# Eight modulation blocks summed on VectorE ahead of TensorE, and Ln and Exp of two scan directions in one instruction

## The chip, the cores and the metric

The kernel runs on one core of one Trainium2 chip. The metric is the device time of one execution in microseconds; for the kernel before it is the median of three runs, 1372.58 us (1371.57 to 1374.09).

## The reference, cut to what matters

Two layers of a hybrid backbone run over 128 context tokens and 256 sample tokens with shared weights. Each layer takes six modulation vectors from the conditioning, one set for the context tokens and one for the sample tokens:

```
mod = silu(c) @ w_mod[l] + b_mod[l]            # c: (1024,), w_mod[l]: (1024, 6 * 1024); for c and for c_ctx
sh1, sc1, g1, sh2, sc2, g2 = split(mod, 6)
h = rms_norm(x, g_pre_mix) * (1 + sc1) + sh1
x = x + g1 * rms_norm(mixer(h), g_post_mix)
h = rms_norm(x, g_pre_ffn) * (1 + sc2) + sh2
x = x + g2 * rms_norm((silu(gate) * up) @ w_ffn_out, g_post_ffn)    # gate, up = split(h @ w_ffn_in), 2816 each
...
a = exp(log_a);  u = sqrt(-expm1(2 * log_a)) * i * x                # RG-LRU, two directions, width 1024
h_t = a_t * h_{t-1} + u_t
```

All tensors are float32.

## The kernel before

The program lays out one core's whole work by hand: each engine has its own stream, written once for each of two layers, and the engines meet at counting semaphores. `Steps` gives each event a label and `at(engine, label)` the value to wait for.

**Weights.** `plan_loads` lists every weight load in the order in which SP issues it. A load is one tile of 128x1024 (two chunks of 128 rows by 512 columns). A split load goes to one of three `raw` buffers; ScalarE writes its rounded part (`highs`, L1106, to `weight_high`), VectorE the rest (`lows`, L1475, to `weight_low`), five slots each. SP waits for the low of the load three before (L529). TensorE then makes three products per block, high by high (L642), high by low activations (L649) and low by high (L650), for 384 tokens at once. A job such as `fi3` is four loads: eight chunks of four 128-column blocks, into four banks. Jobs alternate between two sets of four banks. `token_job` (`wo` and `fo`) has the tokens stationary (L727 to L729).

**FFN stage.** Jobs `fi0` to `fi10` make gate and up blocks, `fo` the output. ScalarE and VectorE, at the end of job j, run two loads ahead (`highs(..., ahead=2)`, `lows(..., ahead=2)`), then `silu` (L1437), `hid` (L1956), the high of `hid` and `hid_low` (L1946). After that VectorE begins with the low of the third load of job j+1.

**Modulation.** The 6 x 1024 columns of `w_mod` are twelve blocks of 512 (r = 0 to 11). The table `MODS` gives each block a host job. Its weights come in four quarters of two chunks (`mod_weight`, two slots, not split). In a hosting job, after the first and the third load, `mod_products` (L681) puts the two conditioning columns, padded to 32, as stationary side against 128 columns of weights, two quarters at a time, into the 128 columns of the banks that the tokens leave free; the chunks go to four groups of 32 partitions. VectorE copies the banks out (`mod_partial`, L1498), and `mod_fold` (L692) adds the four groups and turns the result into columns, in the third load of a later job (`FOLDED`). Blocks 4, 5, 10 and 11 are the gains g1 and g2: `gain_spread` (L709) spreads them over all partitions as rows, with the bias as one more row that `gain_rows` brings. Blocks 0 to 3 (`NEXT`) are those of the next layer, made in the FFN stage of the layer before (not in layer 1, `hosts`); 10 and 11 are needed at the end of the same stage.

**RG-LRU stage.** For each 128 channels and each direction ScalarE makes `t = exp(2 log a)`, `a = exp(log a)` (L1271, L1272), VectorE `squared_root` = (t + 1) tau (L1704), ScalarE the root as Ln and Exp with scale 0.5 (L1277, L1282), VectorE the scans (`scans`, L1679 to L1693). In `lru_coefficients` round e issues the two exponentials of direction e, the Ln of direction e - 1, the last Exp of direction e - 2, and then, in rounds 1, 3, 5, 7 and 9, the high of a weight load. It runs twice a layer, for channels 0 to 3 and 4 to 7. TensorE meanwhile runs `gg0`, `gg1` with gate blocks between them (L857 to L859), then `m2a` and on.

## Time and profile before

| | |
|---|---|
| median of three runs | 1372.58 us |
| the profiled execution: time, span | 1374.85 us, 1373.0 us |
| mean granted TensorE clock | 0.985 |
| busy: TensorE, VectorE, ScalarE | 1310.7, 737.2, 663.6 us |
| L681, hosted modulation products | 1280 records, 43.2 us busy |
| L1475, weight lows | 282, 319.0 us |
| L1106, weight highs | 282, 273.8 us |
| DMA | 196.27 MB, mean 143 GB/s |

One execution is profiled. Busy is the time in which at least one instruction of the engine runs; matmuls overlap, so the pace of TensorE is read from the distance of starts, not from durations. A row of the timeline gives the start, the time from there to the end of the last of its instructions, and in brackets the idle time ahead of it and what ended that. A matmul of float32 operands leaves two records.

### The profile page before, as it was taken

The page shows a single profiled execution, that of the slowest core. Times are in us where ns is not written, and L with a number is a line of the kernel's source. Part 1 is how long each engine was busy: PE and PEld are TensorE (multiplying, and loading weights), DVE is VectorE, ACT ScalarE, POOL GpSimd, SP SyncE. Part 2 cuts the span into 40 slices and gives each one's busy share as a digit, 9 for nine tenths or more (in the row PEclk, how much of TensorE's full clock was granted, in tenths as well). Part 3 has the DMA queues.
Part 4 walks back from the last instruction along what each step waited for, and adds up shares of the span by engine and source line. Part 5 has one row for each costly group of instructions (what it writes and reads, how often), then busy time and mean ns, then how long its engine had stood idle before and what let it go on. Part 6 is the DMA issues. An engine that isn't in the chain of part 4 may idle for free.

```text
span 1373.0 us, 20857 instructions
## 1 busy us (share of the span) xinstructions
PE 1310.7 (95%) x8171; PEld 1196.0 (87%) x8171; DVE 737.2 (54%) x1306; ACT 663.6 (48%) x1199; POOL 18.2 (1%) x38
## 2 busy tenths in 40 slices
PE   5999999998999999999999989999989999999998
PEld 4898899877879999998789988998777899999886
DVE  2687484753754444333367785747447643444424
ACT  4378864743363333332265878637343633333322
POOL 0000000200000000000000000002000000000000
PEclk9999999999999999999999999999999999999999
DMA  9544545313325555535325444453124253445522
GB/s 340 167 139 128 192 138 189 124 61 123 110 91 189 185 184 180 163 134 185 98 85 154 128 158 155 153 191 136 48 77 152 63 158 124 133 151 178 184 97 73
DMA packets 135061, 196.27 MB, mean 143 GB/s; under 512 B 9730, under 2 KB 68268, under 8 KB 134964
## 3 DMA queue, kind: packets, MB, share of 16 engines
q1 hardware_dynamic: 134964, 194.94, 43.4%
q8 instruction: 65, 1.06, 0.3%
q14 instruction: 32, 0.26, 0.1%
HBM read 193.03 MB, written 1.88 MB: 142 GB/s over the span
## 4 chain that ended last, share of the span: by engine, by line
PE 81%; DVE 8%; ACT 6%; DMA 3%; issue 2%; SPq 0%; DVEq 0%; ACTq 0%
PE bank L642 16%; PE bank L649 16%; PE bank L650 15%; PE bank L727 6%; PE bank L729 6%; PE bank L728 6%; PE bank L681 3%; DVE weight_low L1475 2%; ACT weight_high L1106 2%; PE bank L605 2%; PE bank L1015 1%; PE bank L1039 1%; PE bank L709 1%; DVE lru_h L1683 1%; DMA raw<-in_w_o_mla 1%
## 5 line engine op out<-in xcount | busy, mean ns | idle before, releaser
L649 PE MATMUL bank<-act_low,weight_high 128*128 128x384 f32 x1440 | 490.4, 341 | 1.6 <-DVE weight_low L1475 0.9
L650 PE MATMUL bank<-act_high,weight_low 128*128 128x384 f32 x1440 | 485.2, 337 | 0.0
L1475 DVE TENSOR_TENSOR weight_low<-raw,weight_high 128x1024 fp32r<-128x1024 f32 (+5 forms) x282 | 319.0, 1153 | 251.4 <-ACT weight_high L1106 250.3
L1106 ACT ACTIVATE weight_high<-raw 128x1024 fp32r<-128x1024 f32 (+5 forms) x282 | 273.8, 995 | 298.4 <-DMA raw<-in_w_ffn_in 84.2
L642 PE MATMUL bank<-act_high,weight_high 128*128 128x384 f32 x1440 | 324.2, 346 | 6.6 <-ACT weight_high L1106 4.5
L649 PEld LDWEIGHTS bank<-act_low,weight_high 128*128 128x128 f32 x1440 | 273.9, 190 | 8.9 <-issue 4.2
L650 PEld LDWEIGHTS bank<-act_high,weight_low 128*128 128x128 f32 x1440 | 273.5, 190 | 0.0
L642 PEld LDWEIGHTS bank<-act_high,weight_high 128*128 128x128 f32 x1440 | 256.0, 192 | 17.8 <-issue 9.1
L727 PE MATMUL bank<-weight_high,hid_high 128*128 128x512 f32 x264 | 104.4, 395 | 0.0
L729 PE MATMUL bank<-weight_high,hid_low 128*128 128x512 f32 x264 | 102.8, 389 | 0.0
L728 PE MATMUL bank<-weight_low,hid_high 128*128 128x512 f32 x264 | 102.8, 389 | 0.0
L1956 DVE TENSOR_TENSOR t<-bank,sq 128x384 f32<-128x384 f32 x44 | 24.5, 558 | 123.9 <-PE bank L650 121.0
L1437 ACT ACTIVATE sq<-bank 128x384 f32<-128x384 f32 x44 | 19.3, 490 | 129.7 <-PE bank L650 129.7
L728 PEld LDWEIGHTS bank<-weight_low,hid_high 128*128 128x128 f32 x264 | 49.6, 188 | 11.1 <-issue 1.0
L727 PEld LDWEIGHTS bank<-weight_high,hid_high 128*128 128x128 f32 x264 | 49.6, 188 | 11.1 <-issue 1.0
L729 PEld LDWEIGHTS bank<-weight_high,hid_low 128*128 128x128 f32 x264 | 49.6, 188 | 10.4
L1395 ACT ACTIVATE sq<-bank 128x384 f32<-128x384 f32 (+1 forms) x48 | 20.1, 419 | 64.7 <-PE bank L1024 34.5
L1900 DVE TENSOR_REDUCE negmax<-bank 128x1 f32<-128x384 f32 (+1 forms) x48 | 22.2, 466 | 44.4 <-PE bank L1015 44.1
L681 PE MATMUL bank<-mod_weight,cs 128*32 128x128 f32 x1280 | 43.2, 276 | 0.0
L681 PEld LDWEIGHTS bank<-mod_weight,cs 128*32 128x32 f32 x1280 | 32.5, 109 | 9.9 <-issue 9.9
L1186 ACT ACTIVATE act_high<-t 128x384 fp32r<-128x384 f32 x32 | 16.5, 524 | 48.0 <-DVE t L1545 47.8
L605 PE MATMUL bank<-rstd,x 128*128 128x128 f32 x192 | 30.9, 312 | 8.6 <-ACT rstd L1152 6.8
(221 smaller groups left out, 1512.5 us busy)
## 6 DMA issues: line engine op xcount, KB each, us to landing
raw<-in_w_ffn_in SPq DMA_DIRECT2D x176, 256.0 KB, 3.8
mod_weight<-in_w_mod SPq DMA_DIRECT2D x80, 512.0 KB, 4.8
raw<-in_w_in SPq DMA_DIRECT2D x72, 512.0 KB, 4.3
raw<-in_w_ffn_out SPq DMA_DIRECT2D x44, 512.0 KB, 3.3
first_mod<-in_w_mod SPq DMA_DIRECT2D x4, 2048.0 KB, 14.4
raw<-in_w_o_lru SPq DMA_DIRECT2D x16, 512.0 KB, 3.9
raw<-in_w_out SPq DMA_DIRECT2D x16, 512.0 KB, 3.3
raw<-in_w_o_mla SPq DMA_DIRECT2D x8, 512.0 KB, 6.7
```

The costliest lines, as they stand in the source:

```text
L605: ins = nc.tensor.matmul(turn_bank(job, c)[:, P * a:P * a + P], x[:, a, P * c:P * c + P], rstd[:, P * a:P * a + P], start=True, stop=True)
L642: nc.tensor.matmul(bank(job, g)[:, 0:T], view[0][:, kk, cols], high[:, k, :], start=k == 0, stop=False)
L649: nc.tensor.matmul(o, view[0][:, kk, cols], low[:, k, :], start=False, stop=False)
L650: ins = nc.tensor.matmul(o, view[1][:, kk, cols], high[:, k, :], start=False, stop=k == total - 1)
L681: ins = nc.tensor.matmul(bank(job, b)[32 * q:32 * q + 32, T:512], cs[:, k, :], modw[MIDX[n] % MODR][:, 512 * kk + P * b:512 * kk + P * b + P],
L727: nc.tensor.matmul(o, high[:, k, toks], view[0][:, kk, :], start=k == 0, stop=False)
L728: nc.tensor.matmul(o, high[:, k, toks], view[1][:, kk, :], start=False, stop=False)
L729: ins = nc.tensor.matmul(o, low[:, k, toks], view[0][:, kk, :], start=False, stop=k == 2 * pairs - 1)
L1106: nc.scalar.activation(high, w, ACT.Copy).then_inc(*AC.step())
L1475: nc.vector.tensor_tensor(low, w, high.bitcast(F), ALU.subtract).then_inc(*VE.step())
L1900: nc.vector.tensor_reduce(negmax[:, s % 2:s % 2 + 1], bank("attn", s % 2)[:, 0:n], AX.X, ALU.max, negate=True).then_inc(*VE.step("max", s))
L1956: nc.vector.tensor_tensor(t[c % 2][:, :], bank(f"fi{j}", 2 + g)[:, 0:T], sq[c % 4][:, :], ALU.mult).then_inc(*VE.step("hid", c))
```

## The change

Six blocks leave the list of hosted products: 10 and 11, and 0 to 3 where they are made. Their weights come in the same quarters through the same two slots, three quarters to a job, one behind each of the first three loads of `fi1` to `fi8` (the order is 10, 11, 0, 1, 2, 3; in layer 1 only 10 and 11). VectorE multiplies each chunk of 512 columns by the conditioning value of its row (a scalar for each partition) and adds it to a running total of 128x512, one for each conditioning: four operations a quarter, behind the low of the load in its stream. The totals of 10 and 11 lie in `qkv`, those of 0 to 3 in two halves of `ybuf`, shared by 0 and 2, and by 1 and 3; the first quarter of 2 waits for fold 0, that of 3 for fold 1. TensorE sums over partitions: for the gains `ones` is stationary and the total moves (L709's place); for blocks 0 to 3 each 128 columns of a total are stationary against one column of ones, eight products a fold, in `fi5`, `fi7`, `fi8` and `fi9`. The bias of the gains is added to partition 0 of the totals by VectorE; its rows come with `bias_rows` at the first load of `fi1`.

In `lru_coefficients` the Ln and the last Exp take both directions of a channel block in one instruction of 128x768, in rounds 2, 4, 6 and 8; from round 2 on the first exponential waits for the square that last read its buffer.

```
+MODS = ((6, "qk", "st_qkv"), (7, "gg1", "m2b"), (8, "m2a", "outs"), (9, "m1a", "outs"), (4, "m1b", None), (5, "ol1", None))
+SUMMED = (10, 11, 0, 1, 2, 3)
+SUM_FOLD = {"fi5": 0, "fi7": 1, "fi8": 2, "fi9": 3}
+SUM_AT = {(f"fi{1 + q // 3}", q % 3): (SUMMED[q // 4], q % 4) for q in range(24)}
...
+            if (job, i) in SUM_AT:
+                r, q = SUM_AT[job, i]
+                loads.append(Load(("sum", r), 2, 512, False, [("rows", "w_mod", 2 * q, 2, r * 512, 512, 0)]))
...
+        def total(r, g):
+
+            return qkv_flat[:, 1024 * (r - 10) + 512 * g:1024 * (r - 10) + 512 * g + 512] if r >= 10 else \
+                y_flat[:, 1024 * (r % 2) + 512 * g:1024 * (r % 2) + 512 * g + 512]
...
+                def bias_rows():
+
+                    sp.wait_ge(*at(PE, "spread", 5, 1))
+                    sp.sem_inc(sync_passed, 1)
+                    for r in GAINS["ffn"]:
+                        sp.dma_start(partial[r - 10][0:1, :], A["b_mod"][l:l + 1, 512 * r:512 * r + 512]
+                                     ).then_inc(*gain_full.step(by=16))
+                    gain_full.also("bias")
...
-                        sp.wait_ge(*at(PE, "used", MODL[m - MODR], prev=m < MODR))
+                        sp.wait_ge(*at(VE if LOADS[MODL[m - MODR]].job[0] == "sum" else PE, "used", MODL[m - MODR], prev=m < MODR))
...
+                    if r in NEXT:
+                        pe.wait_ge(*at(VE, "summed", r))
+                        for g in range(4):
+                            for e in range(2):
+                                ins = nc.tensor.matmul(out[:, 2 * g + e:2 * g + e + 1], total(r, e)[:, P * g:P * g + P], ones[:, 0:1],
+                                                       start=False, stop=True, skip_group_check=True)
+                        ins.then_inc(*PE.step("fold", r))
+                        return
...
-                        nc.tensor.matmul(bank(f"{job}_b", 2 + g)[:, :], sel[g][:, :], partial[PARTIAL[r]][:, :], start=True, stop=True
+                        rows, values = (sel[g], partial[PARTIAL[r]][:, :]) if which == "mix" else (ones, total(r, g))
+                        nc.tensor.matmul(bank(f"{job}_b", 2 + g)[:, :], rows[:, :], values, start=True, stop=True
...
+                            if e >= 2:
+                                ac.wait_ge(*at(VE, "squared_root", c - 1, d))
                             nc.scalar.activation(t[e % 2][:, :], r_[:, d, j, :], ACT.Exp, scale=ndecay2[:, k:k + 1]).then_inc(*AC.step())
                             nc.scalar.activation(r_[:, d, j, :], r_[:, d, j, :], ACT.Exp, scale=ndecay[:, k:k + 1]
                                                  ).then_inc(*AC.step("a", c, d))
-                        if 1 <= e <= len(order):
-                            j, d = order[e - 1]
-                            ac.wait_ge(*at(VE, "squared_root", 4 * b + j, d))
-                            nc.scalar.activation(tau[:, d, j, :], tau[:, d, j, :], ACT.Ln, bias=epsc[:, 1:2]
-                                                 ).then_inc(*AC.step("ln", 4 * b + j, d))
-                        if e >= 2:
-                            j, d = order[e - 2]
-                            ac.wait_ge(*at(AC, "ln", 4 * b + j, d))
-                            nc.scalar.activation(tau[:, d, j, :], tau[:, d, j, :], ACT.Exp, scale=0.5
-                                                 ).then_inc(*AC.step("root", 4 * b + j, d))
+                        if e >= 2 and e % 2 == 0:
+                            j = e // 2 - 1
+                            c = 4 * b + j
+                            ac.wait_ge(*at(VE, "squared_root", c, 1))
+                            nc.scalar.activation(tau[:, :, j, :], tau[:, :, j, :], ACT.Ln, bias=epsc[:, 1:2]).then_inc(*AC.step())
+                            ac.wait_ge(*last(l, AC))
+                            nc.scalar.activation(tau[:, :, j, :], tau[:, :, j, :], ACT.Exp, scale=0.5).then_inc(*AC.step("root", c))
...
+                        job = LOADS[n].job
+                        if (job, of_job(job).index(n)) in SUM_AT:
+                            sum_quarter(*SUM_AT[job, of_job(job).index(n)])
+
+                def sum_quarter(r, i):
+
+
+                    n = of_job(("sum", r))[i]
+                    if hosts(l, r):
+                        ve.wait_ge(*at(mod_full[MIDX[n] % MODR], "load", n))
+                        if i == 0 and r in (2, 3):
+                            ve.wait_ge(*at(PE, "fold", r - 2))
+                        for kk in range(2):
+                            w = modw[MIDX[n] % MODR][:, 512 * kk:512 * kk + 512]
+                            for g in range(2):
+                                c = cs[:, 2 * i + kk, g:g + 1]
+                                if 2 * i + kk == 0:
+                                    nc.vector.tensor_scalar(total(r, g), w, c, None, ALU.mult).then_inc(*VE.step())
+                                else:
+                                    ve.wait_ge(VE.sem, VE.count - 1)
+                                    nc.vector.scalar_tensor_tensor(out=total(r, g), in0=w, scalar=c, in1=total(r, g),
+                                                                   op0=ALU.mult, op1=ALU.add).then_inc(*VE.step())
+                    VE.also("used", n)
+                    if i < 3:
+                        return
+                    if r >= 10:
+                        ve.wait_ge(*at(gain_full, "bias"))
+                        own()
+                        for g in range(2):
+                            nc.vector.tensor_tensor(total(r, g)[0:1, :], total(r, g)[0:1, :], partial[r - 10][0:1, :], ALU.add
+                                                    ).then_inc(*VE.step())
+                    VE.also("summed", r)
```

## Rows read from the trace of the kernel before

**Rows 1.** The page: busy time, share of the span and instructions of each engine.

```profile
PE 1310.7 (95%) x8171; PEld 1196.0 (87%) x8171; DVE 737.2 (54%) x1306; ACT 663.6 (48%) x1199; POOL 18.2 (1%) x38
```

**Rows 2.** Windows, FFN stage of layer 0: busy time of each engine, clock, DMA.

```profile
core 0: us, PE busy (x) PEld busy (x) DVE busy (x) ACT busy (x) POOL busy (x), PEclk, DMA share, GB/s
...
410.00:620.00 210.00, 210.00 (x1517) 203.14 (x1516) 90.64 (x134) 71.91 (x97) 0.00 (x0) 1.00 0.53 172
```

**Rows 3.** Timeline of TensorE, rows with idle time: RG-LRU stage and `om0`.

```profile
128.83 1.42 PE L642 MATMUL bank<-act_high,weight_high 128*128 128x384 f32 x4 [2.23 <-ACT weight_high L1106]
...
134.97 0.44 PE L857 MATMUL bank<-xc_high,weight_high 128*128 128x384 f32 x1 [0.78 <-DVE weight_low L1475]
...
359.45 0.45 PE L649 MATMUL bank<-o_low,weight_high 128*128 128x384 f32 x1 [1.46 <-DVE weight_low L1475]
```

**Rows 4.** Timeline of VectorE, FFN stage of layer 1, jobs without modulation blocks.

```profile
1119.48 1.25 DVE L1956 TENSOR_TENSOR t<-bank,sq 128x384 f32<-128x384 f32 x2 [6.87 <-PE bank L650]
...
1122.28 3.50 DVE L1475 TENSOR_TENSOR weight_low<-raw,weight_high 128x1024 fp32r<-128x1024 f32 x3 [0.39 <-ACT weight_high L1106]
...
1136.12 1.25 DVE L1956 TENSOR_TENSOR t<-bank,sq 128x384 f32<-128x384 f32 x2 [6.72 <-PE bank L650]
```

**Rows 5.** Timeline of TensorE around a fold and a hosted group, layer 0.

```profile
476.15 0.85 PE L642 MATMUL bank<-act_high,weight_high 128*128 128x384 f32 x4
...
478.23 0.95 PE L692 MATMUL bank<-mod_fold,mod_partial 128*128 128x2 f32 x8
479.04 0.95 PE L642 MATMUL bank<-act_high,weight_high 128*128 128x384 f32 x4
...
481.24 0.85 PE L642 MATMUL bank<-act_high,weight_high 128*128 128x384 f32 x4
...
485.40 0.85 PE L642 MATMUL bank<-act_high,weight_high 128*128 128x384 f32 x4
...
488.58 0.97 PE L642 MATMUL bank<-act_high,weight_high 128*128 128x384 f32 x4
...
490.79 0.85 PE L642 MATMUL bank<-act_high,weight_high 128*128 128x384 f32 x4
```

**Rows 6.** The chain that ended last: start, length, what.

```profile
237.63 1.68 PE bank L692 x16
...
560.99 1.01 PE bank L681 x32
...
596.73 1.01 PE bank L681 x32
```

**Rows 7.** Groups of instructions by line and shape: count, busy, mean ns, idle before.

```profile
L1277 ACT ACTIVATE lru_tau<-lru_tau,epsc 128x384 f32<-128x384 f32 x32 | 19.4, 606 | 12.8 <-DVE lru_tau L1704 12.8
...
L1592 DVE SCALAR_TENSOR_TENSOR x<-ybuf,sums,x 128x512 f32<-128x512 f32 x24 | 16.9, 743 | 0.0
```

**Rows 8.** Timeline of VectorE, two operations of L1592 back to back.

```profile
695.50 1.41 DVE L1592 SCALAR_TENSOR_TENSOR x<-ybuf,sums,x 128x512 f32<-128x512 f32 x2
```

**Rows 9.** Timeline of VectorE in `fi0`, layer 0.

```profile
422.12 1.22 DVE L1475 TENSOR_TENSOR weight_low<-raw,weight_high 128x1024 fp32r<-128x1024 f32 x1 [0.41 <-ACT weight_high L1106]
...
428.98 1.25 DVE L1956 TENSOR_TENSOR t<-bank,sq 128x384 f32<-128x384 f32 x2 [4.13 <-PE bank L650]
```

**Rows 10.** DMA issues: count, KB each, median us from issue to landing.

```profile
mod_weight<-in_w_mod SPq DMA_DIRECT2D x80, 512.0 KB, 4.8
```

**Rows 11.** Windows after the wait at 128.83; columns as in rows 2.

```profile
129.50:132.40 2.90, 2.90 (x10) 2.65 (x9) 2.87 (x7) 2.90 (x8) 0.00 (x0) 0.50 0.45 112
```

**Rows 12.** Timeline of ScalarE in the first `lru_coefficients` of layer 0.

```profile
126.71 0.61 ACT L1277 ACTIVATE lru_tau<-lru_tau,epsc 128x384 f32<-128x384 f32 x1 [2.66 <-DVE lru_tau L1704]
...
127.64 1.04 ACT L1106 ACTIVATE weight_high<-raw 128x1024 fp32r<-128x1024 f32 x1
```

**Rows 13.** Timeline of VectorE in the same stretch.

```profile
121.14 1.23 DVE L1475 TENSOR_TENSOR weight_low<-raw,weight_high 128x1024 fp32r<-128x1024 f32 x1 [1.58 <-ACT weight_high L1106]
...
128.72 1.23 DVE L1475 TENSOR_TENSOR weight_low<-raw,weight_high 128x1024 fp32r<-128x1024 f32 x1 [1.57 <-ACT weight_high L1106]
...
138.67 1.22 DVE L1475 TENSOR_TENSOR weight_low<-raw,weight_high 128x1024 fp32r<-128x1024 f32 x1
```

More of the change, by code:

```diff
@@ L57 @@
 NB = sum(k for _, k in ROWS_B.values())
-MODS = ((6, "qk", "st_qkv"), (7, "gg1", "m2b"), (8, "m2a", "outs"), (9, "m1a", "outs"), (4, "m1b", None), (5, "ol1", None),
-        (0, "fi0", "fi1"), (1, "fi2", "fi3"), (2, "fi4", "fi5"), (3, "fi6", "fi7"), (10, "fi8", None), (11, "fi10", None))
+MODS = ((6, "qk", "st_qkv"), (7, "gg1", "m2b"), (8, "m2a", "outs"), (9, "m1a", "outs"), (4, "m1b", None), (5, "ol1", None))
+SUMMED = (10, 11, 0, 1, 2, 3)
+SUM_FOLD = {"fi5": 0, "fi7": 1, "fi8": 2, "fi9": 3}
+SUM_AT = {(f"fi{1 + q // 3}", q % 3): (SUMMED[q // 4], q % 4) for q in range(24)}
 HOSTED = {host: r for r, host, _ in MODS}
-FOLDED = {fold: r for r, _, fold in MODS if fold is not None}
+FOLDED = {**{fold: r for r, _, fold in MODS if fold is not None}, **SUM_FOLD}
 PARTIAL = {r: i % 2 for i, (r, _, _) in enumerate(MODS)}
@@ L241, in program @@
         pick = sb("pick", [P, 2])
+        qkv_flat = qkv[:, :, :].rearrange("p c t -> p (c t)")
+        y_flat = ybuf[:, :, :].rearrange("p c t -> p (c t)")
+        def total(r, g):
+            return qkv_flat[:, 1024 * (r - 10) + 512 * g:1024 * (r - 10) + 512 * g + 512] if r >= 10 else \
+                y_flat[:, 1024 * (r % 2) + 512 * g:1024 * (r % 2) + 512 * g + 512]
         sel = [rows_a, rows_b]
@@ L383, in program @@
                 reads.append((VE, "partial", HOSTED[name]))
-            for r, _, fold_job in MODS:
-                if fold_job == name:
-                    reads.append((VE, "mod", r))
+            for r in [r for r, _, fold_job in MODS if fold_job == name] + [r for job, r in SUM_FOLD.items() if job == name]:
+                reads.append((VE, "mod", r))
         names = [n for n, _ in jobs]
@@ L462, in gain_rows @@
                 def gain_rows(which):
-                    for r in GAINS[which]:
+                    for r in GAINS["mix"] if which == "mix" else ():
                         sp.wait_ge(*at(VE, "partial", r))
@@ L518, in _ @@
                         gain_rows("ffn")
+                    if n == of_job("fi1")[0]:
+                        bias_rows()
                     if n == of_job("fi2")[0]:
@@ L699, in gain_spread @@
                     which = "mix" if r in GAINS["mix"] else "ffn"
+                    pe.wait_ge(*at(VE, "partial" if which == "mix" else "summed", r))
                     if r == GAINS[which][0]:
-                        pe.wait_ge(*at(VE, "partial", r))
-                        pe.wait_ge(*at(gain_full, which))
                         if which == "mix":
+                            pe.wait_ge(*at(gain_full, which))
                             pe.wait_ge(*at(VE, "mix", 7))
                     else:
-                        pe.wait_ge(*at(VE, "partial", r))
                         pe.wait_ge(*at(VE, "gain", GAINS[which][0]))
                     for g in range(2):
-                        nc.tensor.matmul(bank(f"{job}_b", 2 + g)[:, :], sel[g][:, :], partial[PARTIAL[r]][:, :], start=True, stop=True
+                        rows, values = (sel[g], partial[PARTIAL[r]][:, :]) if which == "mix" else (ones, total(r, g))
+                        nc.tensor.matmul(bank(f"{job}_b", 2 + g)[:, :], rows[:, :], values, start=True, stop=True
                                          ).then_inc(*PE.step("spread", r, g))
@@ L1477, in lows @@
                         made[0] += 1
+                        job = LOADS[n].job
[27 more added lines that the diff above has]
+                    VE.also("summed", r)
                 jobs_reads = dict(jobs)
                 host_of = {r: host for r, host, _ in MODS}
-                fold_of = {r: job for r, _, job in MODS}
+                fold_of = {r: job for job, r in FOLDED.items()}
+                fold_of.update({r: job for r, _, job in MODS})
                 def scalar_reads(job):
@@ L1677, in scans @@
                         ve.wait_ge(*at(VE, "gated", c, d))
-                        ve.wait_ge(*at(AC, "root", c, d))
+                        ve.wait_ge(*at(AC, "root", c))
                         nc.vector.tensor_tensor(i_[:, d, j, :], i_[:, d, j, :], tau[:, d, j, :], ALU.mult).then_inc(*VE.step())
```

## The prediction

> **What bounds the kernel now.** Read the busy shares first: TensorE is busy 1310.7 us of a span of 1373.0 [rows 1]. The windows view over the FFN stage of layer 0 shows TensorE busy for all of 210 us and VectorE for 90.64 of them [rows 2]; the FFN stage of layer 1 looks the same. So in both FFN stages the time is what TensorE is given to do, and work taken from it counts in full as long as the other engines keep it fed. The rest of the idle lies where TensorE waits for ScalarE and VectorE, the RG-LRU stage among them [rows 3]. The change works at both places.
>
> **Removed from TensorE.** Hosted products: blocks 0 to 3 (only in layer 0, for layer 1) and 10, 11 (in both layers) are eight blocks of two groups each. What a group costs is read from the starts of the L642 foursomes, one for each 128-row chunk of weights. Without a group a job of eight chunks takes 16.64 us, from one `hid` to the next [rows 4], so 2.08 a chunk. With a group between two chunks the starts lie 3.18 apart and the next two 2.21 [rows 5]: 1.10 + 0.13 = 1.23 us. The check: two jobs with two groups but no fold are 596.73 - 560.99 = 35.74 us apart [rows 6], and 2 x 16.64 + 2 x 1.23 = 35.74. Eight blocks x 2 x 1.23 = **-19.7 us**.
>
> **Added to TensorE.** The fold of blocks 0 to 3 now takes 8 products of one column, of different stationary blocks, where it took 4 of two columns. Now one fold of 8 records costs 2.89 - 2.08 = 0.81 in its own chunk and 2.20 - 2.08 = 0.12 in the next [rows 5]; two adjacent folds, 16 records as one new fold has, took 1.68 [rows 6]. The moving side is 1 or 2 columns, so the weight loads set the pace. The increment is 0.84 (half of 1.68) to 0.93: four times 0.88 = **+3.5 us**. The gain spreads keep their number and shape (`ones` for `sel`, two moving tiles for one): nothing.
>
> **Added to VectorE, and whether it hides.** Each quarter is four operations on 128x512: six blocks in layer 0 are 24 quarters, three to a job in fi1 to fi8; layer 1 has eight, in fi1 to fi3. The nearest operation is L1592, the same opcode, shape and kind of scalar: 743 ns alone [rows 7], 1.41 us for two back to back, so 0.67 from start to start [rows 8]. A quarter is 0.74 + 3 x 0.67 = 2.75 us. VectorE's cycle in a job: from the start of `hid` to the first low 2.80 us [rows 4], four lows (three back to back took 3.50, so 1.14 from start to start), and three quarters: 2.80 + 4.56 + 8.25 = 15.61 us against 16.64. It hides with 1.03 us to spare a job; the break-even is 3.09 us a quarter. The four removed copies a block were off the path, and so cost and give nothing.
>
> The Trainium skill ("VectorE: DVE Perf Modes", The DRAIN you can't avoid) speaks against it: the next VectorE operation does not start before the pipeline is empty. The rows show starts 0.67 apart for operations of 0.74, so this trace does not bear that out in full. By the rule a quarter would be 4 x 0.743 = 2.97 us and the spare 0.37 a job, still a hidden cost.
>
> The lateness that VectorE carries: in fi0 the lows of fi1 come at 422.12 and after, `hid` at 428.98 [rows 9]. TensorE's fi0 gets shorter by its two groups (2.46), the lows by the one ahead of them (1.23), and two quarters (5.5) come in between: 422.1 - 1.2 + 2.3 (two lows) + 5.5 = 428.7 against a `hid` due at 426.5, 2.2 late. The two one-row additions of the bias (blocks 10, 11) are about 0.75 each, 1.5 a block; the lateness goes 2.2, 2.7, 3.2 and then falls by 1.0 a job. A low of a job's third load is needed 9.0 us after the job starts (four chunks and the high products) and is there at 2.60 + 1.14, say 3.8, plus the lateness: up to 5.2 is free. No stall.
>
> Transfers: a sum load waits for the quarter two before it on VectorE, which the ring of two slots makes. The tightest pair leaves 6.2 us from release to use; landing takes 4.8 [rows 10] plus 0.45 of issue. Hidden. SP passes `bias_rows` behind a spread of the `wo` job, long done. The wait of `gain_rows` for two partial sums goes; the wait for fi10 that stands behind it was nearly as late, and TensorE has no idle in `fo`: nothing.
>
> **One new wait does not hide.** Block 3 shares its buffer with block 1, and its first quarter (q = 20, behind the low of fi7's third load) waits for fold 1. That fold is issued on TensorE only after the third load of the same job fi7. From fi7's start: six chunks 12.5, fold 1.8: 14.3; VectorE sees it at about 14.5, runs the quarter (2.6) and only then the low of the fourth load (1.2): 18.3. TensorE wants it after its high products, at 14.3 + 0.7 = 15.0. A stall of 3.3 us. What comes next: VectorE is then some 2.6 us late in fi8, within the 5.2. Block 2 has the same wait for fold 0 but reaches it a job earlier in the order, on the last of the quarters run ahead, 12.8 us or later into fi5, and there it costs nothing.
> The idle also costs clock: after 2.23 us of idle the granted clock fell to 0.50 (1.2 of 2.4 GHz) [rows 11], and from 128.83 to the next block at 134.97, less its 0.78 wait, TensorE took 5.36 us [rows 3] for a chunk and two thirds, 20 matmuls of 0.173 = 3.46 at full pace: +1.9. Together **+5.2 us**; ends 3.3 (clock kept) and 7.1 (the stretch at half twice as long).
>
> **Log and root in one.** A Ln of 384 is 606 ns [rows 7]; a pair costs about two thirds of two. ScalarE's busy time is not what counts, its order is: in each round the Ln of the next chunk's first direction waited for VectorE's square (2.66 us at 126.71), and the weight high that TensorE and VectorE need stood behind it, at 127.64 [rows 12]. Now rounds 3, 5 and 7 have no Ln, so that high goes out at about 123.0. Walked through with these durations, VectorE's chain of scans, squares and lows starts 0.2 us later, the two exponentials being issued behind the first pair, but loses its two waits of 1.58 and 1.57 [rows 13]: 2.95 earlier at the low of 138.67. TensorE no longer waits 2.23 at 126.6 [rows 3]; it waits instead at the first gate block, from 130.1 to 132.0, for a low of the gates. Does the clock stay? 1.46 us of idle kept it at 359.45 [rows 3], 2.23 lost it [rows 11]: 1.85 is in the middle. Kept, the gain is 2.95 a layer; lost, 1.9 less, 1.05. I take the middle, 2.0, twice (layer 1 repeats the pattern): **-4.0 us**, ends -2.1 and -5.9. In the second round (channel blocks 4 to 7) TensorE's small idle lies mostly behind a partial sum that this does not move: nothing.
>
> **Sum.** -19.7 + 3.5 + 5.2 - 4.0 = -15.0. The profiled execution took 1374.85 us around its span of 1373.0, and becomes 1359.9; it lies 2.3 above the median 1372.58. The median becomes **1357.6 us**, 1.1% less.
>
> **Rivals.**
> 1. *VectorE becomes the bound in fi1 to fi8.* If a quarter costs 3.5 us (waits between the operations, or contention with the loads), a job takes 17.9, 1.2 too much: the lateness that is free is used up by fi3, then every job without a fold to lengthen it loses 1.2 (fi3, fi4 and fi6 of layer 0, fi3 of layer 1), and what is over the 5.2 is lost once, some 7 us in all: 1364.6. For it: the utilisation of 94% worked out above. Against: pairs at 0.67. Chance 0.14. The Trainium skill's rule above goes this way but stops at 2.97, short of the break-even.
> 2. *The wait for fold 1 is hidden* (a low early enough, or VectorE late anyway): 5.2 less, 1352.4. Only if I have the order wrong. 0.11.
> 3. *Slower than before*: the ring of two slots in the queue of SP. If a sum load takes longer than 5.7 us to land, VectorE waits for it once a job; above 6.7 (the spare used) TensorE pays each further us in nine jobs. To lose 15.0 us the landing must take 8.4, where the mean load in the stage is some 210 GB/s (3.5 MB in 16.64 us) against 172 now [rows 2]. 0.04, with 1373 and more.
> 4. *The LRU part gives nothing*, its wait only moves and the clock falls each time: 4.0 more, 1361.6. 0.07.
> Forecast: 0.64, own range 1353.5 to 1361.5.
>
> The range has to take in rival 4, most of 1 and most of 2: 1351 to 1364. This kernel's measurement tells 0.2% (2.7 us) from no change. Faster 0.93, same 0.03, slower 0.04.
>
> **What would show it.** L681 falls from 1280 to 768 records; the jobs fi1 to fi10 last 16.64, those with a fold (fi5, fi7, fi8, fi9 of layer 0) 18.4; one TensorE wait of about 3.3 us on a weight low in fi7 with a dip in clock behind it, and none in layer 1; sum operations of 0.74 at 0.67 starts; in the RG-LRU stage no wait for a weight high, one of 1.9 before gate block 4. I am wrong if VectorE has no idle ahead of `hid` in fi4 to fi6, or the sum loads appear among the releasers.

## The result, and the profile after

The changed kernel takes **1355.36 us** (median of 4 runs, 1353.12 to 1356.12), the kernel before beside it 1372.07 us (4 runs, 1370.21 to 1374.09). The ratio is 0.987 with a 95% interval of 0.985 to 0.9889: 16.7 us faster, where the prediction said 15.0. The profiled execution took 1355.37 us with a span of 1353.6, so it lies at its median, while that of before lay 2.3 above its own. Between the two profiles there are 19.4 us, then, and that is what the rows below add up to.

The page, busy time, share of the span and instructions (answers [rows 1]):

```profile
PE 1291.9 (95%) x7691; PEld 1184.8 (88%) x7691; DVE 814.7 (60%) x1410; ACT 661.2 (49%) x1167; POOL 18.2 (1%) x38
```

TensorE has 480 instructions and 18.8 us less, VectorE 77.5 us more, ScalarE 2.4 us less. VectorE was given four times what TensorE lost; the question is whether that fits beside TensorE. The windows of the FFN stage of layer 0 (answers [rows 2]), and of the stretch at the wait in `fi7` (answers [rows 11]), columns as there:

```profile
410.00:620.00 210.00, 207.30 (x1186) 203.94 (x1185) 149.53 (x209) 74.24 (x99) 0.00 (x0) 0.98 0.58 184
541.50:548.10 6.60, 5.07 (x16) 5.07 (x17) 6.60 (x9) 0.19 (x1) 0.00 (x0) 0.50 0.55 166
```

VectorE goes from 91 to 150 of 210 us and TensorE stays full but for 2.70. Those 2.70 are one wait, and behind it TensorE runs at a granted clock of 0.50 (1.2 of 2.4 GHz): the second window, which takes in the end of the wait, has 0.50 over its 6.6 us. The timeline of TensorE (answers [rows 3] and [rows 5]), of the RG-LRU stage of both layers and of `fi7`:

```profile
131.36 0.45 PE L888 MATMUL bank<-xc_high,weight_high 128*128 128x384 f32 x1 [1.57 <-DVE weight_low L1505]
...
525.20 0.85 PE L665 MATMUL bank<-act_high,weight_high 128*128 128x384 f32 x4
...
537.68 1.84 PE L717 MATMUL bank<-ones,ybuf 128*128 128x1 f32 x16
539.38 0.94 PE L665 MATMUL bank<-act_high,weight_high 128*128 128x384 f32 x4
...
543.03 0.69 PE L672 MATMUL bank<-act_low,weight_high 128*128 128x384 f32 x1 [2.70 <-DVE weight_low L1505]
545.75 1.48 PE L665 MATMUL bank<-act_high,weight_high 128*128 128x384 f32 x4
...
548.94 0.85 PE L665 MATMUL bank<-act_high,weight_high 128*128 128x384 f32 x4
...
797.90 0.44 PE L888 MATMUL bank<-xc_high,weight_high 128*128 128x384 f32 x1 [1.59 <-DVE weight_low L1505]
...
835.86 2.17 PE L913 MATMUL bank<-sq,ones 128*128 128x384 f32 x6 [2.61 <-ACT t L1304]
```

What to see: (a) `fi7` begins at 525.20; the fold (L717) ends at 539.52, the seventh chunk's high products run, and then TensorE waits 2.70 for a weight low. At half clock the next foursome takes 1.48 where it otherwise takes 0.85. `fi8` begins at 548.94. (b) The gate blocks begin at 131.36 and 797.90, where they began at 134.97 [rows 3] and 811.25, each behind one wait of 1.6; the waits of 2.23 for a weight high are gone. (c) In layer 1 the products at L913 (L882 before) wait 2.61, and 1.02 before. The rows of layer 1 before the change:

```profile
805.11 1.62 PE L642 MATMUL bank<-act_high,weight_high 128*128 128x384 f32 x4 [2.23 <-ACT weight_high L1106]
...
811.25 0.45 PE L857 MATMUL bank<-xc_high,weight_high 128*128 128x384 f32 x1 [0.96 <-DVE weight_low L1475]
...
847.59 2.17 PE L882 MATMUL bank<-sq,ones 128*128 128x384 f32 x6 [1.02 <-ACT weight_high L1106]
```

The timeline of VectorE at that wait, and at later `hid` (answers [rows 4] and [rows 9]):

```profile
425.10 1.25 DVE L2019 TENSOR_TENSOR t<-bank,sq 128x384 f32<-128x384 f32 x2
...
473.40 1.25 DVE L2019 TENSOR_TENSOR t<-bank,sq 128x384 f32<-128x384 f32 x2 [0.19 <-PE bank L673]
...
490.04 1.25 DVE L2019 TENSOR_TENSOR t<-bank,sq 128x384 f32<-128x384 f32 x2 [1.80 <-PE bank L673]
...
508.47 1.25 DVE L2019 TENSOR_TENSOR t<-bank,sq 128x384 f32<-128x384 f32 x2 [1.70 <-PE bank L673]
...
525.11 1.25 DVE L2019 TENSOR_TENSOR t<-bank,sq 128x384 f32<-128x384 f32 x2 [1.26 <-PE bank L673]
...
539.63 0.88 DVE L1525 TENSOR_SCALAR ybuf<-mod_weight,cs 128x512 f32<-128x512 f32 x2 [10.50 <-PE bank L717]
540.43 1.41 DVE L1528 SCALAR_TENSOR_TENSOR ybuf<-mod_weight,cs,ybuf 128x512 f32<-128x512 f32 x2
541.75 2.35 DVE L1505 TENSOR_TENSOR weight_low<-raw,weight_high 128x1024 fp32r<-128x1024 f32 x2
544.02 2.74 DVE L1528 SCALAR_TENSOR_TENSOR ybuf<-mod_weight,cs,ybuf 128x512 f32<-128x512 f32 x4
```

VectorE stood still for 10.50 us until the fold released it, did the four operations of block 3's first quarter, and only then the low (541.75) that TensorE needed. The `hid` operations show the pace. Jobs without a fold are 16.64 apart (490.04 - 473.40, and 525.11 - 508.47), the one with fold 0 is 18.43 (508.47 - 490.04), and VectorE waits 1.26 to 1.80 us for TensorE at each.

In the RG-LRU stage of layer 0, first the timeline of ScalarE (answers [rows 12]), then that of VectorE (answers [rows 13]):

```profile
122.60 1.04 ACT L1137 ACTIVATE weight_high<-raw 128x1024 fp32r<-128x1024 f32 x1
125.23 0.94 ACT L1311 ACTIVATE lru_tau<-lru_tau,epsc 128x768 f32<-128x768 f32 x1 [1.59 <-DVE lru_tau L1767]
```

```profile
125.11 1.22 DVE L1505 TENSOR_TENSOR weight_low<-raw,weight_high 128x1024 fp32r<-128x1024 f32 x1
...
130.09 1.22 DVE L1505 TENSOR_TENSOR weight_low<-raw,weight_high 128x1024 fp32r<-128x1024 f32 x1
...
135.06 1.22 DVE L1505 TENSOR_TENSOR weight_low<-raw,weight_high 128x1024 fp32r<-128x1024 f32 x1
```

The high that stood behind the Ln at 127.64 now goes out at 122.60, ahead of the pair, and the three lows run with no idle ahead of them. The groups by line and shape (answers [rows 7] and [rows 8]) and the load of the sums (answers [rows 10]):

```profile
L1528 DVE SCALAR_TENSOR_TENSOR ybuf<-mod_weight,cs,ybuf 128x512 f32<-128x512 f32 x56 | 38.5, 748 | 0.0
...
L704 PE MATMUL bank<-mod_weight,cs 128*32 128x128 f32 x768 | 25.9, 276 | 0.0
...
L1311 ACT ACTIVATE lru_tau<-lru_tau,epsc 128x768 f32<-128x768 f32 x16 | 14.9, 929 | 4.7 <-DVE lru_tau L1767 4.7
...
L1525 DVE TENSOR_SCALAR ybuf<-mod_weight,cs 128x512 f32<-128x512 f32 x8 | 3.5, 482 | 12.3 <-PE bank L717 12.3
```

```profile
mod_weight<-in_w_mod SPq DMA_DIRECT2D x80, 512.0 KB, 4.5
```

**Where the time went.** The end of each stretch is read from equal points of the two timelines.

| stretch | change, us | from |
|---|---|---|
| RG-LRU, layer 0 | -3.1 | gate block -3.61, of which -0.50 was there at 101 us |
| RG-LRU, layer 1 | -3.1 | gate block 13.35 earlier, the products at 794.17 already 10.25 earlier |
| FFN, layer 0: 12 groups | -14.8 | 12 x 1.23 |
| FFN, layer 0: 4 folds | +3.4 | ten jobs take 178.86; less 10 x 16.64 and the stall, 1.78 a fold, 0.93 before |
| FFN, layer 0: stall in `fi7` | +5.3 | from 525.20 to 548.94 TensorE takes 23.74 for a job of 18.43 |
| FFN, layer 1: 4 groups | -4.9 | ten jobs took 171.34 (1274.18 - 1102.84), now 166.40 |
| rest | -2.2 | below |

Of the rest, -0.5 is the start, +1.6 the longer wait at L913, and some -2 us a faster clock in other stages: leaving out the stretches behind the RG-LRU waits and behind the fold, about 34 us stand at half clock before and 31 after. That leaves about 1.5 us that I could not place.

### The profile page after: what moved, and what is told of

Its sections match the earlier page's. It is cut to its first block, busy times and chain, and to the rows that moved or that the text cites. A ratio compares the mean times of both kernels' runs of the same rounds, so it can differ in the third digit from the quotient of the medians.

```text
span 1353.6 us, 19977 instructions
## 1 busy us (share of the span) xinstructions
PE 1291.9 (95%) x7691; PEld 1184.8 (88%) x7691; DVE 814.7 (60%) x1410; ACT 661.2 (49%) x1167; POOL 18.2 (1%) x38
## 4 chain that ended last, share of the span: by engine, by line
PE 82%; DVE 7%; ACT 6%; DMA 3%; issue 2%; SPq 0%; DVEq 0%; ACTq 0%
PE bank L665 17%; PE bank L672 17%; PE bank L673 16%; PE bank L760 6%; PE bank L758 6%; PE bank L759 6%; DVE weight_low L1505 2%; PE bank L704 2%; PE bank L628 2%; PE bank L1046 1%; ACT weight_high L1137 1%; PE bank L740 1%; DMA raw<-in_w_in 1%; PE bank L1070 1%; ACT sq L1145 1%
## 5 line engine op out<-in xcount | busy, mean ns | idle before, releaser
L665 PE MATMUL bank<-act_high,weight_high 128*128 128x384 f32 x1440 | 320.1, 343 | 2.2 <-ACT act_high L1217 2.2
L1467 ACT ACTIVATE sq<-bank 128x384 f32<-128x384 f32 x44 | 19.4, 490 | 145.5 <-PE bank L673 131.4
L760 PEld LDWEIGHTS bank<-weight_high,hid_low 128*128 128x128 f32 x264 | 49.6, 188 | 10.4
L758 PE MATMUL bank<-weight_high,act_high 128*128 128x512 f32 x96 | 39.0, 407 | 0.0
L628 PEld LDWEIGHTS bank<-rstd,x 128*128 128x128 f32 x192 | 28.2, 219 | 12.1 <-issue 9.0
## 6 DMA issues: line engine op xcount, KB each, us to landing
first_mod<-in_w_mod SPq DMA_DIRECT2D x4, 2048.0 KB, 14.3
```

The costliest lines, as they stand in the source:

```text
L628: ins = nc.tensor.matmul(turn_bank(job, c)[:, P * a:P * a + P], x[:, a, P * c:P * c + P], rstd[:, P * a:P * a + P], start=True, stop=True)
L665: nc.tensor.matmul(bank(job, g)[:, 0:T], view[0][:, kk, cols], high[:, k, :], start=k == 0, stop=False)
L758: nc.tensor.matmul(o, high[:, k, toks], view[0][:, kk, :], start=k == 0, stop=False)
L760: ins = nc.tensor.matmul(o, low[:, k, toks], view[0][:, kk, :], start=False, stop=k == 2 * pairs - 1)
```

## The experiments

Four theories were to be told apart. **T1**, the prediction: the FFN part gives 11, the 5.2 paid for the wait on fold 1 already taken off, and the order on ScalarE gives 4. **T2**: that wait is hidden (VectorE would be late there anyway), so that another place for the fold gives nothing. **T3**: the RG-LRU gain comes from the pairing (one Ln for two), not from the order. **T4**: VectorE is at its limit in `fi1` to `fi8`.

**1. Each part alone.** `lru_only` is the kernel before with ScalarE's loop as changed; `ffn_only` is the changed kernel with that loop as it was:

```diff
-                        if e >= 2 and e % 2 == 0:
-                            ...
-                            nc.scalar.activation(tau[:, :, j, :], tau[:, :, j, :], ACT.Ln, bias=epsc[:, 1:2]).then_inc(*AC.step())
+                        if 1 <= e <= len(order):
+                            ...
+                            nc.scalar.activation(tau[:, d, j, :], tau[:, d, j, :], ACT.Ln, bias=epsc[:, 1:2]
```

> The kernel before with the RG-LRU part alone. Theory: the first gate block of the second half starts 3.3 us earlier in each layer, -6 us, 1366, the modulation products and the FFN stage unchanged. Rival (the wait only moves): under 2 us, 1370 to 1372.

Measured: 1365.48 us (12 runs, 1357.6 to 1370.6), 0.9946 [0.9925, 0.9966] of the kernel before (1372.43 on the same chip): 7.0 us less, where both layers' rows in the full change gave 6.2. Its runs scatter more widely than those of any other version. Its timeline of TensorE has the same wait as the full change:

```profile
130.12 0.45 PE L857 MATMUL bank<-xc_high,weight_high 128*128 128x384 f32 x1 [1.57 <-DVE weight_low L1474]
```

> The change without its part in the RG-LRU stage: Ln and last Exp as before, one direction at a time. Theory (the terms of the sum are independent): -19.7 (products) + 3.5 (folds) + 5.2 (wait for fold 1 and its clock) = -11.0 us against the kernel before, 1361; L857's place keeps its 2.2 us wait for a weight high in both layers, the stall in fi7 stays. Rival (the RG-LRU part gives nothing): the whole gain of 16.7 is here, 1355.

Measured: 1366.27 us (6 runs, 1364.32 to 1368.16), 0.9953 [0.9935, 0.9971]: 5 us more than expected. The steps inside the two FFN stages are those of the full change (a 2.7 us wait in `fi7`, jobs of 16.64). Part of what is missing lies in the RG-LRU stage of layer 1:

```profile
797.55 0.95 PE L665 MATMUL bank<-act_high,weight_high 128*128 128x384 f32 x4 [2.23 <-ACT weight_high L1137]
...
803.70 0.59 PE L888 MATMUL bank<-xc_high,weight_high 128*128 128x384 f32 x1 [1.91 <-DVE weight_low L1506]
...
842.93 2.17 PE L913 MATMUL bank<-sq,ones 128*128 128x384 f32 x6 [2.61 <-ACT weight_high L1137]
```

The wait of 2.23 is there as before, but the clock does not fall behind it; it falls behind the next wait, before the gate block (1.91 instead of 0.96). Up to that block nothing is lost: the row of 797.55 is 7.56 us ahead of its counterpart in the kernel before (805.11), that of 803.70 is 7.55 ahead (811.25). From there to L913 the lead falls to 4.66 (847.59 - 842.93), by 2.9 us: 1.6 is the longer wait at L913 (2.61, before 1.02), 1.3 the stretch at half clock, which before lay ahead of the gate block, where a later TensorE only shortened its next wait. Whether the rest was chance I asked with the same kernel once more:

> The FFN part alone again, which came out at 1366 where the terms gave 1361. Theory (the missing 5 us lie outside the FFN stages, in the RG-LRU stage of layer 1 and in where the stretches of half clock fall, and are a property of this program): 1365 to 1367 again, with a gate block of layer 1 in a stretch of half clock and a wait of 2.6 us at L913 there. Rival (chance of one execution or of one chip): 1361 to 1363.

Measured: 1364.21 us (6 runs, 1362.04 to 1365.3), 0.993 [0.991, 0.995], against 1372.53. That lies between the two ranges expected. The waits in layer 1 came again, and two stretches at half clock in later stages did not: `ffn_only` has a granted clock of 0.55 in 995.40:998.70 and in 1015.90:1019.20, `ffn_repeat` 1.00 in both.

```profile
803.17 0.50 PE L888 MATMUL bank<-xc_high,weight_high 128*128 128x384 f32 x1 [1.93 <-DVE weight_low L1506]
```

So the FFN part alone gives 6.2 and 8.3 us in two measurements, where its terms say 11.0, and the RG-LRU part alone 7.0. Both together give 16.7 (17.6 when measured again, below): 1.4 to 4.5 more than the sum. The 1.3 us of half clock behind the gate block are in the FFN part alone and not in the full change; the 1.6 at L913 are in both, and so explain a shortfall against the terms but not this difference. Two measurements of one kernel on two chips differ by 2.1, so the remainder can't be told from scatter.

**2. The fold of block 1 a job earlier.** One character, in the full change (`fold_early`) and in the FFN part alone (`ffn_early`):

```diff
-SUM_FOLD = {"fi5": 0, "fi7": 1, "fi8": 2, "fi9": 3}
+SUM_FOLD = {"fi5": 0, "fi6": 1, "fi8": 2, "fi9": 3}
```

> The changed kernel with fold 1 in fi6 instead of fi7, nothing else: its total is ready after the first quarter placed in fi6, and the buffer is free before VectorE comes to the first quarter of block 3. Theory: the stall in fi7 (2.7 us idle and the half clock behind it) goes, -5.3 us against the changed kernel, 1350. Rival (VectorE is at its limit and would wait or be late elsewhere): within 1 us of the changed kernel, 1355, with a wait on a weight low in fi6 or fi8.

Measured: 1349.13 us (4 runs, 1347.9 to 1353.02), 0.9833 [0.981, 0.9856]. That is 6.2 us less than the changed kernel's 1355.36, each on its own chip, 5.1 by the two ratios (0.0037 of 1372), and 5.3 less than `lru_unpaired` (below), which costs what the changed kernel does and ran on the same chip. The windows show TensorE without a gap and at full clock from 420 to 600 us; VectorE's `hid` of `fi6`, which now has the fold, and of `fi7`:

```profile
420.00:600.00 180.00, 180.00 (x1060) 179.57 (x1059) 134.26 (x189) 61.59 (x86) 0.00 (x0) 1.00 0.60 188
```

```profile
527.44 1.25 DVE L2019 TENSOR_TENSOR t<-bank,sq 128x384 f32<-128x384 f32 x2 [3.05 <-PE bank L673]
...
544.08 1.25 DVE L2019 TENSOR_TENSOR t<-bank,sq 128x384 f32<-128x384 f32 x2 [1.80 <-PE bank L673]
```

> The FFN part alone with fold 1 in fi6. Theory (the stall in fi7 costs 5.3 whatever else is in the program): 5.3 less than the FFN part alone, 1361, and layer 1 as there. Rival (the positions of the half-clock stretches matter as much): anything from 1355 to 1366.

Measured: 1358.44 us (6 runs, 1354.66 to 1363.03), 0.9889 [0.9865, 0.9913]: 5.8 less than `ffn_repeat` on the same chip. T1's price of the wait (5.2) holds and T2 falls: the same fold, one job earlier, causes no wait of TensorE.

**3. The pairing taken out, the order kept** (`lru_unpaired`):

```diff
-                            nc.scalar.activation(tau[:, :, j, :], tau[:, :, j, :], ACT.Ln, bias=epsc[:, 1:2]).then_inc(*AC.step())
-                            ac.wait_ge(*last(l, AC))
-                            nc.scalar.activation(tau[:, :, j, :], tau[:, :, j, :], ACT.Exp, scale=0.5).then_inc(*AC.step("root", c))
+                            for d in range(2):
+                                nc.scalar.activation(tau[:, d, j, :], tau[:, d, j, :], ACT.Ln, bias=epsc[:, 1:2]).then_inc(*AC.step())
+                            for d in range(2):
+                                ac.wait_ge(AC.sem, AC.count - 1)
+                                nc.scalar.activation(tau[:, d, j, :], tau[:, d, j, :], ACT.Exp, scale=0.5).then_inc(*AC.step())
+                            AC.also("root", c)
```

> The changed kernel with Ln and last Exp again one instruction for each direction, but issued in the new places (both behind the second square, none in the odd rounds). Theory (the order made the gain: no Ln waits ahead of a weight high): within 1.5 us of the changed kernel, 1355 to 1357, no wait of TensorE for a weight high. Rival (the shorter work of the paired instructions made the gain): 5 to 6 us slower than the changed kernel, 1361, the 2.2 us wait is back.

Measured: 1354.42 us (5 runs, 1353.16 to 1359.13), 0.9878 [0.9854, 0.9901]: no loss. Its timeline of ScalarE has the two Ln of 384 in 1.12 us and the following high where the full change has it:

```profile
125.03 1.12 ACT L1312 ACTIVATE lru_tau<-lru_tau,epsc 128x384 f32<-128x384 f32 x2 [1.45 <-DVE lru_tau L1770]
...
126.89 1.05 ACT L1137 ACTIVATE weight_high<-raw 128x1024 fp32r<-128x1024 f32 x1
```

T3 falls: the order is the gain, and the pairing adds nothing that these runs can tell from scatter.

**4. More work on VectorE.** With the early fold, one or two more operations a quarter, whose scalar is zero, so that the totals stay what they were (`one_more`, `two_more`):

```diff
+                        for g in range(1):        # range(2) in two_more
+                            ve.wait_ge(VE.sem, VE.count - 1)
+                            nc.vector.scalar_tensor_tensor(out=total(r, g), in0=w, scalar=cs[:, 2 * i + 1, 2:3], in1=total(r, g),
+                                                           op0=ALU.mult, op1=ALU.add).then_inc(*VE.step())
```

> The early fold, with one more operation of 128x512 in each quarter that adds weights times zero: a quarter goes from 2.74 to 3.41 us, 2.0 us a job, nearly all the 1.80 us of idle that VectorE now shows ahead of hid. Theory (a store of lateness of 5.2 us, and a rate limit): the store is used up after the two jobs with bias additions, 2.0 to 2.5 us of TensorE stall in layer 0 and 2.0 in layer 1, +4 to +8 us with the clock, 1353 to 1357. Rival (VectorE's time is hidden altogether): 1349. Rival (VectorE already sets the pace): 24 + 8 quarters at 0.67, +21 us.

Measured: 1353.21 us (4 runs, 1352.23 to 1356.02), 0.9855 [0.9833, 0.9877], 4.1 more than `fold_early` (3.0 by the ratios), inside the range of the theory. TensorE has one stall in each layer's FFN stage, this in layer 0:

```profile
460.05 0.85 PE L665 MATMUL bank<-act_high,weight_high 128*128 128x384 f32 x4
...
463.40 0.97 PE L665 MATMUL bank<-act_high,weight_high 128*128 128x384 f32 x4 [1.11 <-ACT weight_high L1137]
...
466.19 0.85 PE L665 MATMUL bank<-act_high,weight_high 128*128 128x384 f32 x4
```

The two chunks take 6.14 us for 4.16, 2.0 too much; those at 1126.69 in layer 1 take 6.10, 1.9 too much, and the granted clock stays at 1.00 in both. Both stalls stand behind the two jobs in which VectorE also adds the bias: its `hid` of `fi0`, `fi1` and `fi2` come at 423.36, 441.71 and 460.60, 18.35 and 18.89 apart. The last is 6.9 us later than TensorE's pace would have it (`fi3` begins at 453.81), and TensorE stands still for 1.40 of them (1.11, and 0.29 for the low behind it): about 5.5 us of lateness were free, where the prediction had 5.2.

> As one_more with two operations of zero weight in each quarter: 4.0 us a job, 2.2 more than the idle. Theory: each job without a fold now pays its excess, and the jobs with bias more: some 15 us in layer 0 and 7 in layer 1, +22 us over the early fold, 1371, three to five times what one more costs and not twice. Rival (hidden): 1349. Rival (each operation costs the same): twice the price of one more.

Measured: 1374.78 us (12 runs, 1371.44 to 1377.86), 1.0008 [0.9996, 1.002], 25.7 more than `fold_early` (24.0 by the ratios); 22 were expected. From the start of the stage to the `hid` of `fi10` layer 0 takes 15.8 us longer than in `fold_early` and layer 1 8.8. The first further operation costs 3 to 4 us, the second, on one chip, 21.6. The timelines show the pace, first VectorE's `hid` with one more, then with two, then TensorE with two:

```profile
477.56 1.25 DVE L2023 TENSOR_TENSOR t<-bank,sq 128x384 f32<-128x384 f32 x2
494.52 1.25 DVE L2023 TENSOR_TENSOR t<-bank,sq 128x384 f32<-128x384 f32 x2
```

```profile
488.32 1.25 DVE L2023 TENSOR_TENSOR t<-bank,sq 128x384 f32<-128x384 f32 x2
507.26 1.25 DVE L2023 TENSOR_TENSOR t<-bank,sq 128x384 f32<-128x384 f32 x2
```

```profile
451.31 0.96 PE L665 MATMUL bank<-act_high,weight_high 128*128 128x384 f32 x4 [1.90 <-ACT weight_high L1137]
452.57 0.44 PE L672 MATMUL bank<-act_low,weight_high 128*128 128x384 f32 x1 [0.30 <-DVE weight_low L1505]
```

In both versions no `hid` of `fi0` to `fi7` has idle ahead of it in layer 0. VectorE's own cycle in the jobs shown is 16.96 with one more and 18.94 with two, against 16.64 of TensorE. With one more it is 0.3 over; behind its stall TensorE loses 0.6 us more to that in layer 0 (2.38 and 2.39 for 2.08 at 480.75 and 485.21), so nearly all of the price is the stall behind the two jobs with bias. With two it is 2.3 over, and TensorE pays that job by job. T4 is wrong for the change as made. With one more operation a quarter VectorE has no room left, and with two it sets the pace.

**5. The next wait on the list.** With the early fold, VectorE copies a partial sum before it makes the squares of channel block 4 (`partial_first`); and the changed kernel once more beside it (`after_again`):

```diff
-                squared_roots(4)
                 mod_partial(7)
+                squared_roots(4)
```

> The early fold (fold 1 in fi6), and VectorE copies block 7's partial sum out before the two squares of channel block 4 instead of behind them. Theory: TensorE's wait at L913 (1.1 us in layer 0 and 2.3 in layer 1 of the early-fold run) is the wait for that copy, which stands behind the exponentials of ScalarE; it goes, and with it the half clock behind it in layer 1: 3.4 to 5 us less than the early fold, 344 to 346 above 1000, that is 1344 to 1346. Rival (another chain ends the wait, or the later squares cost as much): within 1 us of the early fold, 1349.

Measured: 1345.58 us (4 runs, 1344.44 to 1345.66), 0.98 [0.9781, 0.9819]. That is what the theory said, and 3.6 us less than `fold_early` (4.5 by the ratios). The wait at L913 is gone in both layers (here layer 1):

```profile
823.02 2.10 PE L913 MATMUL bank<-sq,ones 128*128 128x384 f32 x6
```

> The changed kernel again, on the chip of the three others. Its time here is the one that they are to be set against: 1355, and the early fold's 5.3 us lower.

Measured: 1355.98 us (5 runs, 1351.82 to 1358.72), 0.9878 [0.9856, 0.9899], so 17.6 below its 1373.58. `partial_first` is the fastest version made: 10.4 us below the changed kernel on the same chip.

## Why the prediction was right, point by point

- **Removed groups, -19.7.** Right. Layer 1 is the clean case: ten jobs with four groups fewer and nothing else are 4.94 shorter, 1.235 a group. Layer 0's jobs without a fold last 16.64 as layer 1's do.
- **Folds, +3.5.** Right: 0.93 to 1.78, times four, is +3.4. Sixteen records take the same with one moving column as with two (1.68 us in the chain, in this profile and in [rows 6]; 1.84 and 1.85 in the timelines): the moving width does not set the pace. That the weight loads do was argued and not tested.
- **VectorE hides it.** Right, with more room than was thought. Four operations of 748 ns take 2.74, so 0.66 from start to start; in a block's first quarter two of the four are plain multiplications of 482 ns. A job costs VectorE 16.64 - 1.80 = 14.84 us if it holds such a quarter and 16.64 - 1.26 = 15.38 if not, where the prediction had 15.61: it counted the last operation of a quarter at its full length, though the low behind it starts 2.65 after the quarter does (544.02 to 546.67). Rival 1 (VectorE the bound) fell. The Trainium skill ("VectorE: DVE Perf Modes", The DRAIN you can't avoid) says that the next operation does not start before the pipe is empty, and adds that one that is not held starts earlier; here starts lie 0.66 apart for operations of 0.748, so this trace fits the exception and not the rule.
- **The lateness.** `hid` of `fi0` came at 425.10. Counted back from 473.40 in steps of 16.64 it was due at 423.48, so 1.6 late, and `fi1` and `fi2` 1.4 and 1.6: the predicted 2.2, 2.7, 3.2 were too high, the short first quarters and bias additions of 1.28 for the two among the reasons, and no stall came of them. That some 5 us of lateness are free, `one_more` shows.
- **The wait for fold 1, +5.2.** Right in place, order and size. The fold ended 14.3 us into `fi7`, as worked out (525.20 to 539.52). The idle was 2.70 for 3.3: the quarter that VectorE had to do first is a block's first, and took 2.1 up to the low instead of 2.6. Half clock cost 23.74 - 18.43 - 2.70 = 2.6 for 1.9, its stretch being about twice as long as the one it was priced from. The two errors cancel, which is luck: 5.3. Rival 2 fell by `fold_early`.
- **Log and root, -4.0.** The mechanism was right, the term was mis-sized: the step "I take the middle, 2.0". The wait before the gate block was 1.57 and 1.59 for the predicted 1.85, and the clock stayed at full speed, so that both layers gave the upper value of 2.95 and a little more, 3.1 each. Rival 4 fell. The pairing had no part in it that shows (experiment 3); a Ln of both directions takes 929 ns for two of 606, over three quarters of them and not the two thirds of the prediction. By the Trainium skill ("ScalarE: Activation LUTs", What ACT_TABLE_LOAD costs) an activation whose bias is a pointer takes 280 ns and 0.833 ns an element, by estimate 920 for 768 elements; the trace agrees with 929.
- **Transfers.** Right: no wait of any engine names a sum load, landing took 4.5 (the median of all 80 `mod_weight` loads) of the 6.2 us that were free. Rival 3 fell.
- **What the sum left out, -2.2 in the profile.** It priced the clock only where it put a wait. The half-clock stretches of other stages moved too, and the wait at L913 in layer 1 grew by 1.6. `partial_first` shows what removes that wait: VectorE's copy of a partial sum ahead of the squares. What makes it grow stands on ScalarE, which waits twice for a `raw` load shortly before, first after the change, then before it:

```profile
825.60 1.06 ACT L1137 ACTIVATE weight_high<-raw 128x1024 fp32r<-128x1024 f32 x1 [1.50 <-DMA raw<-in_w_in]
828.35 1.06 ACT L1137 ACTIVATE weight_high<-raw 128x1024 fp32r<-128x1024 f32 x1 [1.69 <-DMA raw<-in_w_in]
```

```profile
838.72 1.06 ACT L1106 ACTIVATE weight_high<-raw 128x1024 fp32r<-128x1024 f32 x1 [1.29 <-DMA raw<-in_w_in]
840.07 1.06 ACT L1106 ACTIVATE weight_high<-raw 128x1024 fp32r<-128x1024 f32 x1 [0.30 <-DMA raw<-in_w_in]
```

The two together are 3.19 and 1.59, the wait at L913 2.61 and 1.02. In all eleven profiles that have the wait it is shorter than these two by the same 0.55 to 0.58 (`lru_only` 1.85 and 1.29, `fold_early` 2.86 and 2.29, `ffn_only` 3.18 and 2.61), so each later landing is passed on in full. Why these loads land later with the FFN part is open: SP issues them at the same distance in both kernels (1.0 us behind two `mod_weight` loads), and no experiment took that landing alone.

Against the median the result is 2.2 below the forecast: the RG-LRU term was 2.2 too small (-6.2 for -4.0), and the FFN terms came out as they stood (11.0). The other 2.2 of the profiles do not show in the medians, since the profiled execution of the kernel before lay 2.3 above its median. That the sum of the parts measured alone is smaller stays open in part, as experiment 1 says: the FFN part alone never gave its 11.0.

## What to carry to other kernels

When work goes from a full engine to a half-idle one, its price, as long as it fits, is not its busy time but the order it takes there: of 77.5 us more on VectorE none delayed TensorE but one quarter of a block, which waited for a fold in front of a low and cost 5.3. Look in each in-order stream for the wait that stands in front of something urgent, and move its releaser one job earlier before making anything faster. And price each wait twice, with the clock kept and with the clock lost: the 2.70 us in `fi7` cost as much again at half clock, the 1.6 us before the gate blocks did not, and neither did the 2.61 at L913, so that the length of a wait alone did not tell which it would be.

## What the runs showed of the hardware

- Idle of 1.57 and 1.59 us left the granted clock of TensorE at 1.00; idle of 2.23 (before, layer 0) and 2.70 lowered it to 0.50, and so did 1.90 and 1.81, each with 0.30 soon behind it, in `two_more` (0.52 in 453.90:456.60, 0.51 in 474.60:477.00). But the length of one idle doesn't decide alone. In layer 1 of `ffn_only` TensorE ran on at full clock after an idle of 2.23, and the clock fell after the 1.91 that followed 6 us later; `ffn_repeat` shows the same. At L913 of layer 1 an idle of 2.61 left the clock at 1.00 in the changed kernel, while one of 2.29 lowered it in `fold_early`, where the same six records take 3.87 instead of 2.17:

```profile
835.80:839.00 3.20, 3.14 (x10) 1.98 (x11) 1.56 (x2) 3.17 (x7) 0.00 (x0) 1.00 0.35 78
```

```profile
831.97 3.87 PE L913 MATMUL bank<-sq,ones 128*128 128x384 f32 x6 [2.29 <-ACT t L1304]
```

- What a stretch at half clock costs is not one value: 1.3 us behind the gate block of `ffn_only`, 2.6 in `fi7`.
- A spare of 1.3 to 1.8 us a job on VectorE was enough for a full TensorE over 180 us (clock 1.00, busy 180.00 in `fold_early`). With one operation more a quarter, the cost of 3 to 4 us over both layers came nearly all from the two jobs with bias, in which VectorE's cycle was 18.35 and 18.89; with two more, and a cycle 2.3 us over TensorE's, it was 24 to 26.
- Adding a row of 512 values on one partition (L1537, `tensor_tensor`) takes 676 ns, nearly what the multiply-add takes on all 128 partitions (L1528, 748).
